# V sums of a PEER layer: gather steps of 32 tokens with four slots each, all summed on TensorE, in place of 128 tokens with one slot

## The reference, cut to what matters

```
xn = rmsnorm(x); z = xn @ w_in
a  = conv_branch(hb, hc, hh)                    # 3 taps
b  = diff_attn(q, k, v)                         # 8 heads, QK-norm, rotary, chunk-causal mask
x  = x + (sigmoid(gA) * (a @ w_conv_out) + sigmoid(gB) * (b @ w_attn_out)) @ w_o
xt = rmsnorm(x)
q  = rmsnorm((xt @ wq).reshape(n, 8, 256)) ...  # 8 heads x 2 halves
s_top, i_top = top_k(q @ subkeys, 16)           # of 128 keys, for each half
best, sel    = top_k(sums of pairs, 16)         # 16 experts of a head
g  = softmax(best).reshape(n, 128); e = experts.reshape(n, 128)
h  = gelu(einsum('nkd,nd->nk', u[e], xt))
x  = x + einsum('nk,nkd->nd', g * h, v[e])      # the V sums
```

## Time and profile before

| | |
|---|---|
| median of 3 runs | 3896.55 us (3895.53 to 3901.53) |
| the profiled execution, its time | 3896.9 us |
| its span | 3895.1 us |
| mean granted clock of TensorE | 0.874 |
| TensorE, busy share | 81% |
| VectorE | 65% |
| ScalarE | 37% |
| GpSimd | 38% |
| gathers, queue q0 | 1108.54 MB, 70.3% of 16 DMA engines' span |
| all DMA | 1340.70 MB |

### The profile page before, as it was taken

One profiled execution on the slowest core, in us unless ns is written; L12 is line 12 of the kernel. 1 busy time (PEld: TensorE's weight loads), 2 busy tenths in 40 slices (PEclk: granted clock), 3 DMA queues, 4 the chain that ended last, 5 costly groups with the idle time before them and its releaser, 6 DMA issues.

```text
span 3895.1 us, 46444 instructions
## 1 busy us (share of the span) xinstructions
PE 3173.3 (81%) x14521; PEld 1453.2 (37%) x14521; DVE 2521.7 (65%) x5855; ACT 1459.1 (37%) x4432; POOL 1480.8 (38%) x1410
## 2 busy tenths in 40 slices
PE   6999997888987999797788787878779666666666
PEld 3555554434443554353333333545335111111111
DVE  3333006988888864778777786886578754556664
ACT  2222002356754244222556565234323333333333
POOL 2111001355654433424454554443353433344442
PEclk9999998889998999898889898888889766666676
DMA  4322336799999999998899999999999999999998
GB/s 160 101 87 83 116 100 240 303 366 368 417 386 393 411 417 393 397 359 327 330 355 387 364 366 410 414 416 418 391 419 416 384 420 419 420 419 420 410 419 345
DMA packets 252964, 1340.70 MB, mean 344 GB/s; under 512 B 27344, under 2 KB 66032, under 8 KB 117296
## 3 DMA queue, kind: packets, MB, share of 16 engines
q0 software_dynamic: 152400, 1108.54, 70.3%
q1 hardware_dynamic: 95472, 215.95, 15.1%
q10 hardware_dynamic: 4848, 13.24, 0.9%
HBM read 1310.49 MB, written 27.15 MB: 343 GB/s over the span
## 4 chain that ended last, share of the span: by engine, by line
PE 46%; DMA 24%; DVE 14%; ACT 7%; issue 4%; DVEq 2%; POOL 1%; ACTq 1%; SPq 0%; POOLq 0%
DMA mix<-in_peer_uv,tl_idx 12%; DMA ringx<-in_peer_uv,tl_idx 9%; PE tl_ps L1037 9%; PE tl_ps L983 9%; PE tl_ps L816 7%; PE tl_ps L1020 4%; PE tl_ps L964 4%; PE tl_ps L996 3%; PE tl_ps L881 3%; DVE ringx L1669 3%; PE tl_ps L791 2%; DVE mix L1669 2%; PE tl_ps L850 2%; DMA ringx<-in_peer_uv,tl_itop 2%; DVE tl_xa L1680 2%
## 5 line engine op out<-in xcount | busy, mean ns | idle before, releaser
L737 POOL DMA_INDIRECT mix<-in_peer_uv,tl_idx x512 | 615.4, 1202 | 903.0 <-PE tl_ps L1037 534.9
L737 POOL DMA_INDIRECT ringx<-in_peer_uv,tl_idx x512 | 605.3, 1182 | 855.9 <-PE tl_ps L1037 529.2
L1669 DVE CUSTOM_DVE_ANT_0 mix<-mix,tl_xb 128x1024 f32<-128x1024 f32 x528 | 641.4, 1222 | 291.7 <-DMA mix<-in_peer_uv,tl_idx 263.0
L1669 DVE CUSTOM_DVE_ANT_0 ringx<-ringx,tl_xb 128x1024 f32<-128x1024 f32 x528 | 641.0, 1222 | 280.7 <-DMA ringx<-in_peer_uv,tl_idx 249.5
L1037 PE MATMUL tl_ps<-ringx,tl_dg 64*64 64x512 f32 x3352 | 574.8, 770 | 269.6 <-ACT tl_dg L1267 266.9
L1037 PE MATMUL tl_ps<-mix,tl_dg 64*64 64x512 f32 x3288 | 560.4, 766 | 256.9 <-ACT tl_dg L1267 239.6
L1256 ACT ACTIVATE tl_hg<-tl_hd 128x1 f32<-128x1 f32 x1056 | 213.4, 202 | 1463.5 <-DVE tl_hd L1669 1447.5
L983 PE MATMUL tl_ps<-tl_xr,low 128*128 128x384 f32 (+1 forms) x1280 | 402.2, 471 | 5.2 <-DVE tl_xr L1627 5.2
L1037 PEld LDWEIGHTS tl_ps<-ringx,tl_dg 64*64 64x64 f32 x3352 | 105.0, 155 | 615.8 <-ACT tl_dg L1267 534.0
L1260 ACT ACTIVATE tl_hw<-tl_hg,tl_gw 128x1 f32<-128x1 f32 x1024 | 301.5, 294 | 72.8 <-issue 3.3
L1037 PEld LDWEIGHTS tl_ps<-mix,tl_dg 64*64 64x64 f32 x3288 | 102.9, 155 | 593.0 <-ACT tl_dg L1267 492.1
(11 more groups left out here) (205 smaller groups left out, 3855.3 us busy)
## 6 DMA issues: line engine op xcount, KB each, us to landing
low<-in_wall SPq DMA_DIRECT2D x240, 512.0 KB, 3.6
low<-in_watt SPq DMA_DIRECT2D x60, 512.0 KB, 8.3
mix<-in_peer_uv,tl_idx POOLq DMA_INDIRECT x512
ringx<-in_peer_uv,tl_idx POOLq DMA_INDIRECT x512
ringx<-in_watt SPq DMA_DIRECT2D x12, 512.0 KB
tl_u<-in_x_prompt SPq DMA_DIRECT2D x8, 512.0 KB
x_rows<-tl_u SPq DMA_DIRECT2D x8, 512.0 KB, 7.9
xs_rows<-tl_u SPq DMA_DIRECT2D x8, 512.0 KB
```

The lines of the kernel that those rows point to most:

```text
L737: nc.gpsimd.indirect_dma_start(out=ring[q % RING].rearrange("p a d -> p (a d)"), out_offset=None, in_=A["peer_uv"], in_offset=bass.Indirec ...
L1669: nc.vector.tensor_tensor_reduce(out=ring[q % RING][:, 0, :], in0=ring[q % RING][:, 0, :], in1=xb[:, t % 2, :], scale=1.0, scalar=0.0, op0 ...
```

## The change

Every gather step now has 32 tokens with four slots each, as the sample tile had before. A pass is the 32 tokens (a group `g`) of a tile; it has 32 steps, but in tile 0 passes of 8 steps go round the four groups (`place`, `PASSES`; 45 passes in all). Partition `32 b + r` of a step holds token `r` of the group and its slot of number `b`.

- V sums: all 1056 steps on TensorE. The diagonal is 128x32, one 32x32 identity below the other, so a matmul with it adds the four slots of a token too. Four pieces of 256 columns each go to four strips of 32 columns of the array and four quadrants of PSUM (`sums(g, b)`). `by_dve`, `add_row`, `SHARED`, `add_start` and the fold at the end are gone; VectorE adds the 128x256 sums of each pass to `xa` (`add_sums`, 33 times).
- x rows: the dot product needs a group's 32 normed rows in all four quadrants. `load_row` brings them once by DMA (32x1024), and ScalarE copies them into the three other quadrants (`repeat_row`, 135 copies in all, L1319), a pass ahead, in steps 3, 4 and 5 of every eight-step or longer pass.
- Indices and gates are written for 128 tokens and then spread over the quadrants by small VectorE copies (`by_quadrants`, L1434; 16 for a prompt unit, 592 in all for indices and gates).
- The `x1` rows of a tile come, and `y` is stored, as four DMAs, one for a quadrant.
- In `attend(0)` the three convolution blocks of a head have places of their own (`CV` is now 1.2, 3.6, 6.2 in a unit of 7): the first ahead of the projection of its unit, the second behind it, the third behind `turn_weights`.
- Numbers such as 3 and 24 are replaced by functions of `TILES` and `UNIT0`, keys, values and turned heads are held in a ring of six units, the turned normed rows are stored at block 16 of the first middle instead of block 50, ScalarE's exponentials of the gates are run last in a step, and `PLAN` and `UNIT_AT` have slightly other places.

```diff
+TOKS = P // QUAD
+COLS = D // QUAD
...
-PV, TO, PJ, TQ, CV = 1.0, 5.0, 2.6, 0.8, 3.6
+PV, TO, PJ, TQ, CV = 1.0, 5.0, 2.6, 0.8, (1.2, 3.6, 6.2)
-SHARED = ((0,170,1,6),(170,300,3,4),(336,520,1,6),(520,680,2,3))
...
-def by_dve(q):
+def place(q):
     t, k = divmod(q, SLOTS)
-    if not (4 if t == 0 else 14) <= k < SLOTS - 4:
-        return False
-    return any(first <= q < end and q * share % whole < share for first, end, share, whole in SHARED)
-def ndve(q):
-    return sum(by_dve(i) for i in range(max(q, 0)))
-def npe(q):
-    return max(q, 0) - ndve(q)
+    if t == 0:
+        return t, k // 8 % QUAD, k // 32 * 8 + k % 8
+    return t, k // TOKS, k % TOKS
+def pass_length(t):
+    return 8 if t == 0 else TOKS
+PASSES = [(k, 0, k // 8 % QUAD) for k in range(0, SLOTS, 8)] + [(k, k // SLOTS, k % SLOTS // TOKS) for k in range(SLOTS, NT * SLOTS + TOKS, TOKS)]
+PASS_AT = {first: p for p, (first, t, g) in enumerate(PASSES)}
...
-                    if npe(q + 1 - RING) > npe(q - RING):
-                        pool.wait_ge(s["used_pe"], npe(q + 1 - RING))
-                    else:
-                        pool.wait_ge(s["used_dve"], ndve(q + 1 - RING))
+                    pool.wait_ge(s["used_pe"], q + 1 - RING)
...
-                        last = nc.tensor.matmul(ps[:, (3, 5, 3)[k], 0:nr], w[:, c, :], xn[:, c, 0:nr], start=(c == 0), stop=(c == DC - 1))
+                        last = nc.tensor.matmul(ps[:, (3, 5, 5)[k], 0:nr], w[:, c, :], xn[:, c, 0:nr], start=(c == 0), stop=(c == DC - 1))
...
+                    if here and rb == 0 and i == 0:
+                        for pos in conv_block(g, 0):
+                            yield step_at(rb, u, pos)
...
             def weigh(q):
-                t, k = divmod(q, SLOTS)
-                pe.wait_ge(s["dg_done"], npe(q) + 1)
-                if k == 0 and t:
-                    pe.wait_ge(s["part_done"], t)
-                elif k == 0:
-                    pe.wait_ge(s["n_cp"], 6)
-                for b, h in quarters:
-                    rows = half_of(b)
-                    last = nc.tensor.matmul(ps[half_of(h), b, :], dg[rows, npe(q) % DIAGS, :],
-                                            ring[q % RING][rows, 1, h * 512:(h + 1) * 512], start=k == 0,
-                                            stop=t == NT and k == DEC - 1, skip_group_check=True)
+                t, g, j = place(q)
+                pe.wait_ge(s["dg_done"], q + 1)
+                if q == 0:
+                    pe.wait_ge(s["n_cp"], REST)
+                elif j == (0 if t else 24) and QUAD * t + g > 1:
+                    pe.wait_ge(s["summed"], QUAD * t + g - 1)
+                for b in range(QUAD):
+                    last = nc.tensor.matmul(sums(g, b), dg[:, q % DIAGS, :], ring[q % RING][:, 1, b * COLS:(b + 1) * COLS],
+                                            start=j == 0 and g < 2, stop=j == TOKS - 1, skip_group_check=True)
                 last.then_inc(s["used_pe"], 1)
...
-            def add_start(t):
-                pe.wait_ge(s["xa_in"], 16 * (t + 1))
-                if ndve((t + 1) * SLOTS):
-                    pe.wait_ge(s["used_dve"], ndve((t + 1) * SLOTS))
-                for b, h in quarters:
-                    rows = half_of(b)
-                    last = nc.tensor.matmul(ps[half_of(h), b, :], ident[rows, rows], xa[rows, h * 512:(h + 1) * 512],
-                                            start=False, stop=True, skip_group_check=True)
-                last.then_inc(s["summed"], 1)
...
-                gate = nc.scalar.activation(hw[:, j:j + 1], hg[:, j:j + 1], ACT.Copy, scale=table(gw, tops, t)[:, k:k + 1])
-                if by_dve(q):
-                    gate.then_inc(s["hw_done"], 1)
-                else:
-                    act.drain()
-                    if npe(q) >= DIAGS:
-                        act.wait_ge(s["used_pe"], npe(q) - DIAGS + 1)
-                    nc.scalar.activation(dg[:, npe(q) % DIAGS, :], eye[:], ACT.Copy, scale=hw[:, j:j + 1]).then_inc(s["dg_done"], 1)
+                nc.scalar.activation(hw[:, j:j + 1], hg[:, j:j + 1], ACT.Copy, scale=gw[:, t % 2, k:k + 1])
+                act.drain()
+                if q >= DIAGS:
+                    act.wait_ge(s["used_pe"], q - DIAGS + 1)
+                nc.scalar.activation(dg[:, q % DIAGS, :], eye[:], ACT.Copy, scale=hw[:, j:j + 1]).then_inc(s["dg_done"], 1)
...
+            def load_row(p):
+                first, t, g = PASSES[p]
+                act.wait_ge(s["xs_out"], 16 * TILE0[BLOCK_OF[t] + 1])
+                act.dma_start(xb[quadrant(0), p % 2, :], A["xs"][t * P + g * TOKS:t * P + (g + 1) * TOKS, :]).then_inc(s["row_in"], 16)
+            def repeat_row(p, b):
+                act.wait_ge(s["row_in"], 16 * (p + 1))
+                nc.scalar.copy(xb[quadrant(b), p % 2, :], xb[quadrant(0), p % 2, :]).then_inc(s["rows_done"], 1)
...
+            def by_quadrants(dst, src, t, h0, nh):
+                n = QUAD * nh
+                for g in range(1 if t == NT else QUAD):
+                    first = h0 // 2 * 32 + g * 8 if t == 0 else g * TOKS + QUAD * h0
+                    for b in range(QUAD):
+                        nc.vector.tensor_copy(dst[quadrant(b), t % 2, first:first + n], src[quadrant(g), b * n:(b + 1) * n])
...
-            def add_row(q):
-                t, k = divmod(q, SLOTS)
-                dve.wait_ge(s["hw_done"], ndve(q) + 1)
-                dve.wait_ge(s["xa_in"], 16 * (t + 1))
-                if ndve(q):
-                    dve.wait_ge(s["used_dve"], ndve(q))
-                nc.vector.scalar_tensor_tensor(out=xa[:], in0=ring[q % RING][:, 1, :], scalar=hw[:, k % TOPK:k % TOPK + 1],
-                                               in1=xa[:], op0=ALU.mult, op1=ALU.add).then_inc(s["used_dve"], 1)
+            def add_sums(q):
+                t, g, j = place(q)
+                dve.wait_ge(s["used_pe"], q + 1)
+                if g == 0:
+                    dve.wait_ge(s["xa_in"], 64 * (t + 1))
+                nc.vector.tensor_tensor(xa[:, g, :], ps[:, g % 2, g // 2 * COLS:(g // 2 + 1) * COLS], xa[:, g, :],
+                                        ALU.add).then_inc(s["summed"], 1)
...
+                if q >= EVICT and place(q - EVICT)[2] == TOKS - 1:
+                    add_sums(q - EVICT)
+            add_sums(LAST - 1)
```

796 lines of the change are left out of this document (409 added, 387 removed).

## The result

The changed kernel takes 3937.89 us, median of 4 runs (3930.92 to 3946.68), against 3897.19 us of the kernel before. The ratio is 1.0107, with a 95% interval of 1.0095 to 1.0119: 1.1% slower, where 0.9% faster was forecast. The profiled execution took 3946.68 us, 9 us more than the median, with a span of 3944.5 us. The traces of the two kernels are therefore 49.4 us apart where the medians are 40.7 apart.

What follows compares the result with a forecast made beforehand. The prediction took DMA as the bound from the first gather on, with 105 us idle. Terms -5, +2, +7, -8, -8, -20, -1 and -4 gave -37 from 3896.9: 3860 us, 0.9% faster, range 3800 to 3905 (about 0.8).

Steps and rivals of the forecast that it cites:

- From the first gather on the DMA engines are the bound.: After 646 us: DMA sets the pace; lighter TensorE or VectorE only fills its idle time, 105 us in all.
- TensorE gets 77 us of 610 back there, where it is the most loaded: 1790 to 2400 us: 157 steps took 187 us on TensorE; all 183 at 0.6 would take 110.
- the sum put down at -1: 1230 to 1700 us and the tail: of 13 us idle, tile boundaries without TensorE's wait for a sums copy give 1.
- 0.57: V-sum step at full clock: four column strips running at once take 0.57 us, half of the old 1.09.
- VectorE's copies, +2 and +7: 16 index copies before the first `idx_ready`: +2; 646 to 760 us, copies +15 and six adds fewer -8: +7.
- I cost that wait at nothing: ScalarE's x row copies waiting for `row_in`: transfers land in 3.7 to 7.1 us, three slots are 7.7 or more.
- the rival with 0.07: Attention stretches: ScalarE's copies delay TensorE, 57 copies of 1.01 us, +58 against -37, ending at 3918; chance 0.07.
- The relief, -36 in the attention stretches: 820 to 1230, 1700 to 1790, 1790 to 2400 us: half of DMA's idle time filled, -8, -8, -20.
- Before the first gather -5 and +2: First attention: convolution block covers TensorE's 0.75 us wait in seven heads, -5; 16 index copies before `idx_ready`, +2.
- The end, -4: After the last dot product, 11.4 us before: shorter V sum, add and four stores replace copy, eight matmuls and add, -4.
- The clock: Rival: lighter TensorE gets a lower clock; in 1790 to 2400 at 0.68, 90 against 77 us, ending at 3910; chance 0.04.
- the relief at 46 with 9 of cost: Whole sum: gains -5, -8, -8, -20, -1, -4 and costs +2, +7, together -37.

Runs made afterwards that it cites:

- both cuts: Changed kernel with 94 steps from 170 to 299 at 8 V-sum columns instead of 1024, and 4 table copies of 128 partitions instead of 16 of 32: 3857.4 us.
- the short copies: Changed kernel with ScalarE's x row copies 8 instead of 1024 columns long from the third pass on: 26.3 us less than the changed kernel.
- e7: Changed kernel with VectorE taking 94 V sums between steps 170 and 299 into a buffer that TensorE folds in once a pass: 3905.1 us.
- e5: Kernel before, with the V sums of steps 170 to 299 all on TensorE in its old 64x64 pieces: 91 us slower than the kernel before.
- e3: Changed kernel with 4 copies of 128 partitions instead of 16 of 32 per index or gate table (148 instead of 592): 43.9 us less than the changed kernel.

## Why the prediction was wrong

The steps of the prediction in their order.

- *"From the first gather on the DMA engines are the bound."* This failed, and the rest hangs on it. The shares of the earlier trace rows were read as how full the engines are. In 1230 to 1700 the share was 1.00 with TensorE busy 446 of 470 us; in steps 192 to 288 both were at their limit at once (TensorE 321.6 of 323.1 us, 404 GB/s where 409 is the most that a run reached there), and the run that gave TensorE 85 more V sums lost all of their time. A share of 0.98 stood beside 370 GB/s after.
- *V sums, "TensorE gets 77 us of 610 back there, where it is the most loaded".* The count of steps on either engine came from 1790 to 2400 alone, where VectorE did 26 of 183. It had 85 of the 130 steps from 170 to 299. There, in the stretch that the sum put down at -1, 130 steps at 0.64 us stand for 45 at 1.09: 83 - 49 = +34. Steps 128 to 288 took 26.1 us longer, and leaving out 94 of these V sums gave 39.4. This is the step that failed by most, with the copies below close behind it. That a step takes 0.64 us and not 0.57 is 9 of the 83.
- *VectorE's copies, +2 and +7.* Mis-sized and misplaced. One takes 0.18 us for 0.13, which was the mean of 0.09 and 0.18, and VectorE's load costs time up to step 128, not only to 760 us, which is step 27: cut to a quarter they gave 43.9 us, 24.1 of it in steps 0 to 128. VectorE need not be full for that: in steps 64 to 128 it is busy 162.6 of 211.4 us.
- *ScalarE's copies, "I cost that wait at nothing".* The wait for the rows was small indeed (5.5 us), but the copies' own time had been put at zero in the sum: 26.3 us. This was the rival with 0.07. It was right on the place, the attention stretches, and left out half of those who wait: VectorE waits for ScalarE there as well as TensorE.
- *The relief, -36 in the attention stretches.* Some is there: with both cuts the kernel came at 3857, 40 us under the kernel before, with ScalarE's copies still in it. In the changed kernel it shows as -22.4 in steps 288 to 384; the -10.4 in 128 to 192 has in it the 24 dense matmuls that moved behind step 192. That it is half of the idle time, as the forecast took it, no run shows.
- *Before the first gather -5 and +2.* The waits for the turned heads in the first attention went down as reckoned, 15.0 us before:

```profile
PE tl_ps L816 <- ACT tl_u L1148: 15.0, 20, 0.8
```

and after:

```profile
PE tl_ps L854 <- ACT tl_u L1171: 10.2, 14, 0.7
```

The first dot product starts 1.7 us later all the same, between 648.6 and 654.2 us in the fourteen traces, so neither term can be told from no change there. (The first gather starts 1.8 us later, where 2 to 5 us earlier was forecast.)
- *The end, -4.* Right: 7.3 us for 11.4.
- *The clock.* The granted clock fell from 0.98 to 0.93 in steps 64 to 128 and from 0.67 to 0.54 in the tail. The tail's steps take the same 2.56 us, since TensorE waits there. Elsewhere no run separates the clock from the rest.

The account: both cuts gave 3857; less the 26 of the short copies it would be 3831, an estimate, since the three were not run together. Against that number the change costs 39 for V sums where TensorE is full, 44 for index and gate copies and 26 for x rows, and relieves 66, which is what is left over and was not measured by itself. The forecast had the relief at 46 with 9 of cost. What stays open: which waits the relief comes of; in steps 384 to 512, why fewer copies gave some 16 us where VectorE is only 9.6 us lighter; and what makes the other half of the 17 us between like kernels there, beside the wait for the weights.

## What to carry to other kernels

Before an engine is called light, multiply its busy share out by stretch, and where an engine is within a percent of the stretch's length it is a bound, also when another is at its limit too: work given to it there costs its full time. A hand-made table that splits work unevenly over the stretches says where that is; count its entries per stretch, not its mean. And a layout change that saves on a large operation should be charged for the many small ones that feed it: here 592 copies of 0.18 us, 135 of 1.04 and the V sums in the one stretch where TensorE is full ate the gain. Such a charge holds for the stretch where it was measured: copies of VectorE cost their whole time up to step 128, and 236 fewer, most of them behind it, gave 0.4 us.

## What was not expected of the hardware

- The DMA share stays near 1 when the rate falls: 0.98 at 370 GB/s, 1.00 at 404, 1.01 at 409. From the packets in the traces, one of 8 KB of the gathers takes in steps 192 to 288 on average 0.320 us at 409 GB/s (e7), 0.322 at 404 (before), 0.344 at 370 (after) and 0.357 at 332 (e5).
- Four matmuls of 128 rows by 32 columns in four strips of the array run side by side: eight instructions of 256 columns in 0.64 us at full clock, 1.08 at half.
- A VectorE copy of 32 partitions by 8 or by 16 elements takes the same 0.17 to 0.18 us. Copies that each write another quadrant start 0.18 us apart, a pair within one quadrant 0.09, and the 148 copies of all 128 partitions in e3 take 16.5 us together, 0.11 each.
